# Differential attention with joint scores on disjoint rows, normalised probabilities transposed and values stationary on two column groups

## The reference, cut to what matters

```python
def diff_attention(...):                       # kind A; A_QK = 32, A_V = 64, two maps c per head
    s = einsum('bqhcd,bkhcd->bhcqk', q, k) * (A_QK ** -0.5)
    p = softmax(s, axis=-1)
    a = p[:, :, 0] - lam * p[:, :, 1]
    o = einsum('bhqk,bkhd->bqhd', a, v)
    o = rmsnorm(o, subln_g) * (1.0 - lam_init) # over the 64 features of a head
def neighbourhood_attention(...):              # kind B; head width 64, bias on the 512 latent keys
    p = softmax(concatenate([s_win + bias, s_ctx]), axis=-1)
    ol = p_win @ v_rows + p_ctx @ vc
xl = xl + g1_l * (concatenate([a_l, b_l, p_l, h_l], axis=-1) @ w_out)
```

## Time and profile before

| | us |
|---|---|
| median of 3 runs | 2429.42 (2428.84 to 2431.74) |
| profiled execution, its own time | 2430.29 |
| its span | 2428.4 |
| attention stage, first scores to first matmul of L1345 | 257.0 to 430.4, 173.4 |
| busy in 257.0 to 430.4: PE, DVE, ACT, POOL | 160.8, 117.7, 96.9, 83.4 |
| the 13 steps between the scores of step 2 and of step 15 | 273.8 to 406.9, 133.1 |

### The profile page before, as it was taken

The page is one execution under the profiler, slowest core; times in us unless marked ns, Lnnn a source line. Parts: engine busy times, 40 slices in busy tenths (PEclk is TensorE's granted clock), DMA queues, the critical chain, the costliest instruction groups (busy, mean ns, idle before and its releaser), DMA issues.

```text
span 2428.4 us, 28708 instructions
## 1 busy us (share of the span) xinstructions
PE 2296.2 (95%) x10070; PEld 1621.4 (67%) x10071; DVE 950.8 (39%) x1775; ACT 529.4 (22%) x1101; POOL 187.9 (8%) x181
## 2 busy tenths in 40 slices
PE   8999999867799898999999999999999999999999
PEld 2554566422333377678888888566676788888888
DVE  5532566430000135725335432444244434335421
ACT  3200465411111144522111100131231212111100
POOL 0000435011111100000000002202010000000000
PEclk9999999878899999989999999999999999999999
DMA  9221152659786931012222221312112122222230
GB/s 345 85 98 33 48 203 107 240 187 378 271 341 244 354 124 53 27 53 78 87 85 81 77 97 59 131 43 86 61 59 79 35 104 79 87 88 87 77 120 19
DMA packets 81023, 298.02 MB, mean 123 GB/s; under 512 B 8990, under 2 KB 8990, under 8 KB 80431
## 3 DMA queue, kind: packets, MB, share of 16 engines
q1 hardware_dynamic: 75102, 271.26, 31.6%
q0 software_dynamic: 5840, 25.67, 2.9%
HBM read 282.73 MB, written 14.16 MB: 122 GB/s over the span
## 4 chain that ended last, share of the span: by engine, by line
PE 87%; DVE 4%; ACT 2%; issue 2%; SPq 2%; DMA 2%; DVEq 0%; POOL 0%; ACTq 0%; POOLq 0%
PE products L1606 41%; PE products L992 8%; PE products L1436 6%; PE products L1216 6%; PE products L1511 3%; PE products L1454 3%; PE products L1770 2%; PE products L1267 2%; PE products L1688 2%; PE products L1345 1%; PE products L1561 1%; PE products L1280 1%; PE products L1235 1%; PE products L1256 1%; DMA weights_and_work<-in_experts 1%
## 5 line engine op out<-in xcount | busy, mean ns | idle before, releaser
L1606 PE MATMUL products<-normed,weights_and_work 128*128 128x264 f32 (+1 forms) x1520 | 348.7, 384 | 0.0
L1606 PEld LDWEIGHTS products<-normed,weights_and_work 128*128 128x128 f32 x1520 | 288.1, 190 | 50.7 <-issue 5.3
L1436 PE MATMUL products<-weights_and_work 128*64 128x512 f32 x768 | 181.3, 633 | 48.8 <-DMA weights_and_work<-in_experts 48.1
L1861 ACT ACTIVATE weights_and_work<-products 128x256 f32<-128x256 f32 (+3 forms) x221 | 95.6, 452 | 407.4 <-PE products L1606 156.4
L1606 PE MATMUL products<-weights_and_work,mixed 128*128 128x256 f32 (+1 forms) x800 | 182.3, 382 | 0.8 <-ACT weights_and_work L1861 0.8
L1436 PEld LDWEIGHTS products<-weights_and_work 128*64 128x64 f32 x768 | 65.6, 146 | 162.9 <-issue 161.2
L1606 PEld LDWEIGHTS products<-weights_and_work,mixed 128*128 128x128 f32 x800 | 151.8, 190 | 24.4 <-ACT weights_and_work L1861 1.6
L1606 PE MATMUL products<-weights_and_work 128*128 128x256 f32 (+1 forms) x672 | 151.0, 385 | 7.2 <-DVE residual L3238 5.2
L1606 PE MATMUL products<-weights_and_work,normed 128*128 128x264 f32 (+1 forms) x704 | 155.6, 382 | 0.0
L1606 PE MATMUL products<-normed,mixed 128*128 128x264 f32 (+1 forms) x672 | 154.1, 382 | 0.0
L1606 PEld LDWEIGHTS products<-weights_and_work 128*128 128x128 f32 x672 | 128.8, 192 | 28.1 <-issue 7.3
(11 more groups left out here) (562 smaller groups left out, 2959.4 us busy)
## 6 DMA issues: line engine op xcount, KB each, us to landing
weights_and_work<-in_weights SPq DMA_DIRECT2D x301, 512.0 KB, 4.3
weights_and_work<-in_experts SPq DMA_DIRECT2D x192, 512.0 KB, 5.4
results<-normed SPq DMA_DIRECT2D x8, 512.0 KB, 7.1
residual<-in_x POOLq DMA_DIRECT2D x1, 2048.0 KB, 15.3
weights_and_work<-in_dft_half POOLq DMA_DIRECT2D x1, 2048.0 KB, 14.1
token_rows<-mixed SPq DMA_DIRECT2D x4, 512.0 KB, 3.1
normed<-results SPq DMA_DIRECT2D x4, 512.0 KB, 6.8
mixed<-results SPq DMA_DIRECT2D x4, 512.0 KB, 7.3
```

The costliest lines, as they stand in the source:

```text
L1436: m = pe.matmul(ps[UNIT * b:UNIT * (b + 1), side, :], job_t[:, k, UNIT * b:UNIT * (b + 1)], expert_w[b][:, s, at:at + 512], start=(k == 0) ...
L1606: m = pe.matmul(bank(p, n), left(k), right(k), start=(fresh and k == 0), stop=(k == kt - 1), skip_group_check=True)
L1861: act.activation(out, src, ACT.Copy, scale=scale).then_inc(bank_free[p.bank], 1)
```

## The change: joint scores, normalised probabilities, stationary values, feature-major output

- **Scores.** A head of kind A and the head of kind B whose operands lie in the other 64 rows of the array (`h ^ 1`) are scored in one sequence of six matmuls: A map 0 (32 rows, 512 columns), B (64 rows, 512), A map 1 (32 rows, 512), A map 0 (256), B (256), and after the wait for `half_scored` A map 1 (256). All five score banks must be free before it begins.
- **Probabilities.** A's maps are scaled by their inverse sums and joined into a separate buffer (`joined_a`), B's are scaled into another (`scaled_b`), both on VectorE before the transposes. ScalarE's copies of the products are then plain.
- **Weighing.** The values are stationary (128 rows, 64 columns) and the transposed probabilities move (128 columns). A's output goes to PSUM partitions 0 to 63 and B's to 64 to 127 of the same bank, so the product is feature-major. One copy of 128x128 takes both to `mix`; the rows of the projection's weights are permuted to fit, on the host.
- **Norm.** A's outputs are squared by ScalarE (64x512), summed over partitions by one matmul, and the root is taken on 64x512. VectorE's `head_norm` works in place in `mix`. The transposes of `feature_major` are gone.
- **Buffers.** `plan()` gives bank 6 to the weighed product of step `s-1` ahead of the second half of A's transposes of step `s`.

The core of the diff follows; its four loops over the steps are, in this order, those of `plan()`, TensorE, ScalarE and VectorE.

```diff
+            r["scores", s, "B"] = b.take(3, 4)
+            r["scores", s, "A"] = b.take(0, 1, 2)
+    scores(0)
     for s in range(len(STEPS)):
-        scores(s + 1, "A")
-        turned(s, "A")
-        weighed(s - 1, "B")
-        scores(s + 1, "B")
-        turned(s, "B")
+        scores(s + 1)
+        if s > 0:
+            r["PV", s - 1] = b.take(6)
+        for kind in "AB":
+            r["T", s, kind] = [b.take(5), b.take(6)]
         if s % 2 == 1:
             r["out_1", s // 2] = b.take(7)
-        weighed(s, "A")
-        if s in OUT_AT:
-            r["OT", OUT_AT[s]] = [b.take(5), b.take(6)]
+        if s in SUMMED_AT:
+            r["o_sum", SUMMED_AT[s]] = b.take(5)
...
+                    fill(b_)
+                    fill(a)
+                    def first(c, at, key, width):
+                        rows_ = slice(o + 32 * c, o + 32 * c + 32)
+                        return pe.matmul(wide(a, 2 * NKEY)[:, at:at + width], aq[rows_, h // 2, t * P:(t + 1) * P],
+                                         ak[rows_, h // 2, key:key + width], start=True, stop=True)
+                    def second(at, width):
+                        rows_ = slice(DH - o, 2 * DH - o)
+                        return pe.matmul(wide(b_, NKEY)[:, at:at + width], bq[rows_, h // 2, t * P:(t + 1) * P],
+                                         bk[rows_, h // 2, at:at + width], start=True, stop=True)
+                    m = first(0, 0, 0, 512)
+                    second(0, 512)
+                    first(1, 1024, 256, 512)
+                    first(0, 512, 512, 256).then_inc(half_scored, 1)
+                    finish(b_, second(512, 256))
+                    pe.wait_ge(half_scored, s + 1)
+                    finish(a, first(1, NKEY, 0, 256))
...
-                        m = pe.matmul(ps[:, p.bank, 0:DH], prob_t[:, a, kt, :], vals[:, kt, a, h * DH:(h + 1) * DH],
-                                      start=(kt == 0), stop=(kt == NKT - 1))
+                        for a, head in ((0, h), (1, h ^ 1)):
+                            m = pe.matmul(ps[DH * a:DH * (a + 1), p.bank, 0:P], vals[:, kt, a, head * DH:(head + 1) * DH],
+                                          prob_t[:, a, kt, :], start=(kt == 0), stop=(kt == NKT - 1), skip_group_check=True)
...
+                def summed(t):
+                    p = r["o_sum", t]
+                    fill(p)
+                    pe.wait_ge(sub_squared, t + 1)
+                    finish(p, pe.matmul(ps[0:DH, p.bank, :], head_ones[0:DH, 0:DH], o_root, start=True, stop=True))
...
                 for s in range(len(STEPS)):
-                    scores(s + 1, "A")
+                    scores(s + 1)
+                    if s > 0:
+                        weigh(s - 1)
                     turn(s, "A")
                     out_1(s, 0)
-                    if s > 0:
-                        weigh(s - 1, "B")
-                    scores(s + 1, "B")
                     turn(s, "B")
                     out_1(s, 1)
-                    weigh(s, "A")
-                    if s in OUT_AT:
-                        feature_major(OUT_AT[s])
+                    if s in SUMMED_AT:
+                        summed(SUMMED_AT[s])
...
                 for s in range(len(STEPS)):
-                    turned(s, "A")
+                    if s - 1 in SUMMED_AT:
+                        sums(SUMMED_AT[s - 1])
                     exps(s + 1, "A")
                     if s > 0:
-                        weighed(s - 1, "B")
-                    turned(s, "B")
+                        weighed(s - 1)
+                    turned(s, "A")
+                    if s in SUMMED_AT:
+                        squares_a(SUMMED_AT[s])
                     exps(s + 1, "B")
-                    weighed(s, "A")
-                    if s % HEADS == 0 and s > 0:
-                        roots(s // HEADS - 1)
+                    turned(s, "B")
+                    if s - 1 in SUMMED_AT:
+                        roots(SUMMED_AT[s - 1])
...
                     link(dve.reciprocal(inv[:, 0:2], sums[:, 0:2]))
-                    link(stt(inv[:, 1:2], inv[:, 1:2], neg_lam, sums[:, 0:1], ALU.mult, ALU.mult))
-                    stt(prob_a[:, 0], prob_a[:, 1], inv[:, 1:2], prob_a[:, 0], ALU.mult, ALU.add).then_inc(prob_ready, 1)
+                    link(ts(inv[:, 1:2], inv[:, 1:2], neg_lam, None, ALU.mult))
+                    if s > 0:
+                        ready(dve, r["T", s - 1, "A"][1])
+                    ts(joined_a, prob_a[:, 0], inv[:, 0:1], None, ALU.mult).then_inc(prob_scaled, 1)
+                    dve.wait_ge(prob_scaled, s + 1)
+                    stt(joined_a, prob_a[:, 1], inv[:, 1:2], joined_a, ALU.mult, ALU.add).then_inc(prob_ready, 1)
...
                 for s in range(len(STEPS)):
                     joined(s)
+                    scaled_by_sum(s)
+                    maxima(s + 1, "A")
+                    maxima(s + 1, "B")
                     if s % 2 == 0 and s > 0:
                         take_out(s // 2 - 1)
-                    if s in OUT_AT:
-                        head_norm(OUT_AT[s])
-                    maxima(s + 1, "A")
-                    if s % HEADS == 0 and s > 0:
-                        head_squares(s // HEADS - 1)
+                    if s - 2 in SUMMED_AT:
+                        head_norm(SUMMED_AT[s - 2])
                     mod2_term(2 * s)
-                    read(dve, r["scores", s, "B"])
-                    dve.reciprocal(row_inv[:, s % 2, 2:3], row_sum[:, s % 2, 2:3]).then_inc(inv_b, 1)
-                    maxima(s + 1, "B")
```

150 lines of the change are left out of this document (61 added, 89 removed).

## The result

Median of 4 runs 2466.19 us (2462.16 to 2467.64) against 2429.13 (4 runs, 2425.87 to 2431.74); ratio 1.0151, 95% interval 1.0133 to 1.0168. The change makes the kernel 37 us slower. 2451 (2417 to 2464) was forecast: the direction was right, the size too small by 15 us, and the time lies 2 us outside the range.

The account below looks back on a forecast made before the run. TensorE was taken to bound the old kernel, and a loop over several engines the changed one. Steps 2 to 15 +13.8, beginning +6.8 and end +1.1 made +21.7, so 2451 us, range 2417 to 2464.

Parts of the forecast that it names:

- Weighing: TensorE in attention: two weighings of 1.49 us become one of 1.47, taking 1.5 us per step off TensorE.
- Scores: TensorE's joint A and B scores: 4.4 us a set, against 3.30 for both sets in the old kernel.
- two bounds: Joint scores: 2.25 us if disjoint rows run side by side, 4.4 if changes between 32 and 64 rows prevent overlap.
- The loop: Loop from A's scores through ScalarE's weighed copy to the next scores: 11.1 us a step, TensorE idling about 2.1.
- The 13 steps: Attention steps 2 to 15: 146.9 us against 133.1, +13.8, including three matmuls that sum squares at 0.86.
- The forecast's own range: Whole kernel: 2442 to 2464 us; below if something overlaps, above if the clock falls in the gaps.
- Beginning: Start of attention, up to the third scores: later maxima, B's exponentials and the low clock, together +6.8 us.
- End: From the last scores to the end of attention, 23.4 us in the old kernel: +1.1 us.
- Side by side, at full clock: Rival on the joint scores: disjoint rows overlap, scores 2.25 us, loop 8.95, kernel 2420 us; chance 0.25.
- Half overlap: Rival on the joint scores: scores about 3.3 us, loop 10.0, kernel 2433.5 us; chance 0.10.
- the second rival: Scores overlap, but TensorE's new gap makes the clock fall: 15 us in 13 steps, kernel 2435 us; chance 0.13.
- The first rival: Rows side by side at full clock, 2420 us, with 3 us (0 to 9) for GpSimd holding VectorE; chance 0.25.

Follow-up runs that it names:

- e2: B's 64-row score matmuls done as two accumulating halves of 32 rows, also changing the order, against the changed kernel; 2426.6 us.
- before: The kernel without the change, the one every run was compared with; median 2429.1 us.
- e4: Both out_1 matmuls of a step put between A's fourth and fifth transpose, against the changed kernel; 2492.0 us.
- e14: Each score matmul over all 128 rows, so the result is not the reference's, against the changed kernel; 2451.7 us.
- e1: A's four score matmuls first in the joint set, then B's two, against the changed kernel; 2436.7 us.
- after: The changed kernel itself, against the kernel without the change; 2466.2 us, ratio 1.0151.
- e3: ScalarE copies the previous step's weighed product ahead of A's exponentials, against the changed kernel; 2470.5 us.
- e15: e4 with each score matmul over all 128 rows, so the result is not the reference's; 2464.2 us.
- e9: e2 and e3 together, plus VectorE's copy of out_1 ahead of A's maxima, against the changed kernel; 2418.1 us, ratio 0.9950 to before.

## Why the prediction was off

- *Weighing:* 1.47 us forecast, 1.46 measured.
- *Scores:* 4.4 us taken from two bounds; 4.41 measured, for the reason given (e2 shows it by taking the change of shape away: 2.70).
- *The loop:* 11.1 us a step forecast, 11.14 measured; TensorE's gap before A's fifth transpose 2.1 and 1.88, released by the copy that was named. The matmuls that sum squares add 1.03 (0.86 forecast).
- *The 13 steps:* +13.8 forecast. At full clock it would have been 13 times 11.15 and 3 times 1.03, 148.0 us: +14.9. Measured +24.2. **The step that failed is the clock's term in this sum, which was nought.** The other 9.3 us stand in the steps in which the clock fell: 44.4 us at half speed would cost 22.2 of work, and TensorE's gaps hid the rest. I had spoken of falls only as coming from gaps. The forecast's own range did reach to 2464 for them, 13 us above the sum, but no term was worked out for them with long scores, and a slower tail "with clock falls on top" was left outside the range. The runs showed another cause that the rows of before could not: seven of the ten falls stand behind scores of 32 or 64 rows one after another, with no gap (TensorE busy for 3.40 of the 3.40 us ahead of each; e4 without the gap has more of them, and in e14 128 rows take 44.4 down to 7.1).
- *Beginning:* +6.8 forecast, +10.5 measured. The sum counted 2 us for the low clock; the second set of scores alone, all of it at 1.2 GHz, took 8.3 us (269.01 to 277.27) instead of 4.4. Here too the clock fell (at 260.8) behind a set of scores, 3.26 us busy of 3.40. In e14 the same stretch took 23.1 us for 27.3, with 10.0 us of low clock for 23.9.
- *End:* +1.1 forecast, +2.2 measured; 5.7 us at low clock there against 4.2. The rest I did not separate.
- *Rivals:* "Side by side, at full clock" did not happen, but e2 built its premise, and A's maxima began 2.39 us in and the loop came out at 9.02 us where 2.4 and 8.95 were worked out; 2426.6 us against 2420, with 10.2 us of low clock left in its steps. "Half overlap" took a set of 3.3 us for a loop of 10.0. e1 has a set of 3.7 and a loop of 8.98: the loop counts to the end of A's scores, which is the end of the set in after alone. That a falling clock could cost some 15 us in 13 steps was priced in the second rival, at nearly the size that was missing, but only for short scores.

## What to carry to other kernels

Matmuls on disjoint rows ran side by side here only where they had the same tile shape. Where one needs 64 rows and the other 32, two halves of 32 rows that accumulate were worth it, though they stream the columns twice: the set of scores went from 4.41 to 2.70 us, and against the better order alone (e1) the kernel gained 10 us, by the clock and not by the loop. Where a change leaves TensorE with narrow matmuls one after another, price the clock at its lower level too, even if the engine never idles: a loop 0.7 us shorter (e3) brought nothing, and a filled gap (e4) made the kernel slower. And when a loop over several engines binds, ask on whose end it hangs (here A's scores, not the set), and then for the next in-order neighbour, such as VectorE's copy of out_1, before a gain is booked.

## What the runs showed of the hardware

- The granted clock fell though TensorE never idled. With matmuls of 32 or 64 rows one at a time it fell behind a stretch of 3.40 us busy out of 3.40 (after), and TensorE was at 1.2 GHz for 102 of 184 us (e4); the same matmuls over 128 rows had 26.8 of 158 us (e15), and 7.1 of 145 us although 1.88 us were idle in each step (e14). With the rows went the changes of shape, as said above.
- A GpSimd instruction held up VectorE's instructions with one input too, not only those with two. In e9, VectorE's scaling of 128x768 with one input (L2539) takes 0.62 us when GpSimd rests, and its sum of two (L2541) 1.02:

```profile
345.46 0.62 DVE L2539 TENSOR_SCALAR weights_and_work<-weights_and_work,tiny 128x768 f32<-128x768 f32 x1
346.12 1.02 DVE L2541 SCALAR_TENSOR_TENSOR weights_and_work<-weights_and_work,tiny 128x768 f32<-128x768 f32 x1
```

Beside GpSimd's two-input instruction they take 2.27 and 2.98, and end 0.4 and 0.8 us after it:

```profile
364.00 3.02 POOL L874 TENSOR_TENSOR normed<-normed 128x1024 f32<-128x1024 f32 x1
365.18 2.27 DVE L2539 TENSOR_SCALAR weights_and_work<-weights_and_work,tiny 128x768 f32<-128x768 f32 x1
375.78 2.52 POOL L874 TENSOR_TENSOR normed<-normed 128x1024 f32<-128x1024 f32 x1
376.15 2.98 DVE L2541 SCALAR_TENSOR_TENSOR weights_and_work<-weights_and_work,tiny 128x768 f32<-128x768 f32 x1
```

The Trainium skill (SBUF — State Buffer, SBUF: two separate sides) says that the port pair shared by VectorE and GpSimd is an exclusive lock that also a VectorE instruction in a two-port performance mode needs; 2.27 against 0.62 agrees, though the trace does not name the mode. It also says that the lock is held for the whole instruction, and there e9 differs for a GpSimd instruction with one input (L872): VectorE's sum takes longer than 1.02 us beside it, but ends 0.9 us before it (by spans of GpSimd that are rough in the profile).

```profile
367.12 3.03 POOL L872 TENSOR_SCALAR normed<-weights_and_work,tiny 128x1024 f32<-128x1024 f32 x1
367.48 1.75 DVE L2541 SCALAR_TENSOR_TENSOR weights_and_work<-weights_and_work,tiny 128x768 f32<-128x768 f32 x1
```

The first rival's hold of 0 to 9 us had counted only instructions with two inputs. The change adds two scalings with one input per step. In e9 the two slowest of the 13 steps (10.59 us for 8.58, and 11.30 for the 9.98 of a step with the summing matmul) are among those with such holds; others with one (at 283.68 and 311.26) stand by steps of 9.27 and 8.66 us, so what a hold costs depends on where it falls.
